# A two-block layer with a mixture of 32 experts: the order of the output projection, the first expert and its ten weight buffers

## The reference

```python
mixed = merged @ w_o
h = _layer_norm(DEEPNORM_ALPHA * h + mixed, ln1_g, ln1_b)       # 512 x 1024
pg = softmax(h @ w_rg + b_rg)                                    # 4 groups
grp = argmax(pg)
le = (h @ w_re + b_re).reshape(512, 4, 8)[token, grp]            # 8 experts of the group
top_v, top_i = top_k(le, 2)                                      # 2 experts a token
for each block of rows of one expert e (32 experts, 1024 -> 512 -> 1024):
    y = (silu(xb @ w1[e]) * (xb @ w3[e])) @ w2[e]
out[token] += gate * y
```

## Time and profile before

| | |
|---|---|
| median of 3 runs | 2123.84 us (2122.33 to 2124.23) |
| the profiled execution | 2123.43 us, of which the profile's span is 2121.6 us |
| PE, DVE, ACT, POOL busy | 92%, 44%, 31%, 21% of the span |
| the experts, from the first gather to the last weight | about 732 to 1226 us |

### The profile page before, as it was taken

The page is one execution under the profiler, slowest core; times in us unless marked ns, Lnnn a source line. Parts: engine busy times, 40 slices in busy tenths (PEclk is TensorE's granted clock), DMA queues, the critical chain, the costliest instruction groups (busy, mean ns, idle before and its releaser), DMA issues.

```text
span 2121.6 us, 23001 instructions
## 1 busy us (share of the span) xinstructions
PE 1958.5 (92%) x9509; PEld 1427.4 (67%) x9509; DVE 930.6 (44%) x1398; ACT 667.6 (31%) x993; POOL 444.4 (21%) x311
## 2 busy tenths in 40 slices
PE   7999999999999699887978899998889999999999
PEld 6788878788878533333333358876767787888887
DVE  6866385724436612111111155445546883222342
ACT  4644532424333101000000133541238752222221
POOL 5542221424325111111111023211003200000121
PEclk9998999999999799988999899999999999999999
DMA  4872462213334699999999964111111134323211
GB/s 165 271 190 61 99 120 40 89 51 80 80 123 189 247 392 403 404 403 397 416 408 411 423 238 139 60 50 50 50 50 40 59 133 136 119 79 119 80 60 40
DMA packets 108310, 369.47 MB, mean 174 GB/s; under 512 B 10682, under 2 KB 43708, under 8 KB 95912
## 3 DMA queue, kind: packets, MB, share of 16 engines
q1 hardware_dynamic: 97456, 343.58, 46.0%
q0 software_dynamic: 8240, 19.00, 2.6%
q10 hardware_dynamic: 2504, 5.35, 0.7%
HBM read 345.03 MB, written 29.15 MB: 176 GB/s over the span
## 4 chain that ended last, share of the span: by engine, by line
PE 75%; DVE 12%; issue 5%; ACT 5%; DMA 2%; POOL 0%; SPq 0%; DVEq 0%; POOLq 0%; ACTq 0%
PE ps L278 71%; PE ps L282 3%; DVE ST L262 3%; PE ps L2210 2%; DVE H L268 1%; ACT ST L274 1%; ACT M L274 1%; ACT L274 1%; DVE ST L1088 1%; DVE WL L262 1%; DVE BG L262 0%; DMA ypad<-BG,yrow 0%; DVE ML L262 0%; DMA BG<-h1d,toki 0%; DVE H L265 0%
## 5 line engine op out<-in xcount | busy, mean ns | idle before, releaser
L278 PE MATMUL ps<-XH,WS 128*128 128x512 f32 x704 | 216.7, 389 | 0.0
L278 PE MATMUL ps<-W,BG 128*64 128x512 f32 x448 | 159.1, 642 | 22.0 <-issue 22.0
L278 PEld LDWEIGHTS ps<-XH,WS 128*128 128x128 f32 x704 | 132.2, 188 | 27.3
L2318 DVE COPY BG<-ps 128x512 f32<-128x512 f32 x32 | 22.1, 692 | 285.5 <-PE ps L278 285.5
L272 ACT ACTIVATE BG<-ps 128x512 f32<-128x512 f32 x48 | 28.6, 595 | 372.3 <-PE ps L2210 336.6
L278 PE MATMUL ps<-ST,BG 128*64 128x512 f32 (+2 forms) x384 | 139.5, 572 | 6.2 <-issue 4.5
L278 PE MATMUL ps<-XL,WS 128*128 128x512 f32 x352 | 137.0, 389 | 1.4 <-DVE XL L262 1.4
L278 PE MATMUL ps<-X2H,GV 128*128 128x512 f32 (+1 forms) x512 | 130.1, 343 | 0.0
L278 PE MATMUL ps<-HTH,WL 128*128 128x512 f32 x448 | 115.6, 395 | 0.0
L278 PE MATMUL ps<-WS,HH 128*128 128x512 f32 x352 | 108.5, 389 | 0.9 <-DVE WS L262 0.9
L278 PE MATMUL ps<-M,BG 128*64 128x512 f32 (+1 forms) x288 | 100.0, 525 | 8.1 <-ACT ST L272 6.4
(11 more groups left out here) (400 smaller groups left out, 4436.2 us busy)
## 6 DMA issues: line engine op xcount, KB each, us to landing
W<-in_w SPq DMA_DIRECT2D x28, 2048.0 KB, 40.7
W<-in_w_in SPq DMA_DIRECT2D x27, 2048.0 KB, 10.1
ST<-in_w SPq DMA_DIRECT2D x19, 2048.0 KB, 42.1
W<-in_w_ffn_in SPq DMA_DIRECT2D x22, 1024.0 KB, 7.7
BG<-in_w SPq DMA_DIRECT2D x10, 2048.0 KB
U<-in_w SPq DMA_DIRECT2D x10, 2048.0 KB, 39.5
...
```

Of the source, the lines that this page charges most:

```text
L278: return p.e.matmul(o, lhsT=l, rhs=r, start=start, stop=stop, skip_group_check=True)
L2318: v.e.tensor_copy(hs[j], t.at).then_inc(t.drained)
```

## The change

It has five parts.

1. Order in `p_merge`: the half y = 0 of all four tiles is computed first, then y = 1. The logits of tiles 0 and 1 now stand inside the last two results, and the turn of a tile follows its y = 1 half. ACT does all copies of turned tiles. The norm of the last tile is written in two halves, and its first transposes wait for the first half alone.
2. Buffers: the fourth buffer (slot 3) is now the region `BG` 8 to 15, which held the split half 0 of `w_o`, instead of `U`, which takes the experts' small tiles. The order of buffers and of the sources is changed so that loads 4 and 5 (now w1 and w3 of expert 1; load 3 is w2 of expert 0) wait only for the last y = 0 result.
3. Expert 0's rows: no gather. DVE makes, ahead of everything else that follows the ranks, a one-hot matrix of expert 0's tokens (`oh0`), and PE gets the transposed rows by 32 float32 products of `H` with it.
4. Order in `p_experts`: eh(0), the list for the overflow rows, et(0), ex(1), ey(0), and only then eh(1).
5. `occupy`: 2, 6 and 1 products of constants ahead of the last logits, the ranks and expert 0's rows.

```diff
@@ -212,7 +212,7 @@
         b_rows = [nc.dram_tensor(f"b_rows{y}", (32, P), F32).ap() for y in range(2)]
-        Wt += [U.rearrange("p a b -> p (a b)"), M.rearrange("p a b -> p (a b)")]
+        Wt += [BG[:, 8:16, :].rearrange("p a b -> p (a b)"), M.rearrange("p a b -> p (a b)")]
         Wt += [ST[:, 2:10, :].rearrange("p a b -> p (a b)"), HT.rearrange("p a b -> p (a b)")[:, 0:4096]]
@@ -342,7 +342,9 @@
                 srcs += [wrows(a["w1"][0, x], 8), wrows(a["w3"][0, x], 8)]
-            if x:
+            if x == 0:
+                srcs.append(wrows(a["w2"][0, 0], 4))
+            elif x > 1:
                 srcs.append(wrows(a["w2"][0, x - 1], 4))
@@ -354,7 +356,7 @@
-        EXP_SLOTS = (5, 1, 7, 2, 0, 3, 4, 6, 8, 9)
+        EXP_SLOTS = (5, 1, 7, 2, 3, 0, 4, 8, 6, 9)
         EXP_LAST = (5, 7, 3, 4, 6, 1)
...
@@ -419,7 +421,11 @@
             v.wait_ge(*v.now)
-            stt(o, o, rs[:, i:i + 1], rows[:, br, :], MUL, ADD).then_inc(ln_hi)
+            if halves:
+                stt(o[:, 0:512], o[:, 0:512], rs[:, i:i + 1], rows[:, br, 0:512], MUL, ADD).then_inc(ln_lo)
+                stt(o[:, 512:], o[:, 512:], rs[:, i:i + 1], rows[:, br, 512:], MUL, ADD).then_inc(ln_hi)
+            else:
+                stt(o, o, rs[:, i:i + 1], rows[:, br, :], MUL, ADD).then_inc(ln_hi)
         def v_ln_high(X, u, i, gr, br, rows_in, rows=rows):
@@ -439,9 +445,12 @@
-        def p_turn(name, X, u, i, banks):
-            p.wait_ge(ln_hi, 4 * u + i + 1)
+        def p_turn(name, X, u, i, banks, first=None):
             for h in range(2):
+                if h or first is None:
+                    p.wait_ge(ln_hi, 4 * u + i + 1)
+                else:
+                    p.wait_ge(*first)
                 t = B.tile((name, i, h), banks[h])
@@ -1737,7 +1746,7 @@
             for m in range(2):
-                t = B.tile(("wo", m, 0), 2 * m)
+                t = B.tile(("wo", m, 0), m)
                 room(t)
@@ -1758,27 +1767,26 @@
-            for m in range(NT):
+            for m, y in [(2, 0), (3, 0)] + [(m, 1) for m in range(NT)]:
                 z = slice(m * P, (m + 1) * P)
-                for y in range(m < 2, 2):
-                    hi, lo = cols8(WO[y]), cols8(WL[slot[20 + y]])
-                    t = B.tile(("wo", m, y), (2 * m + y) % 4)
-                    room(t)
-                    for k in range(8):
-                        p.wait_ge(sp_hi, job["wo", y, k // 2] + 1)
-                        mm(t.at, MH[:, k, z], hi[:, k, :], start=k == 0, stop=False)
-                        mm(t.at, ML[:, k, z], hi[:, k, :], start=False, stop=False)
-                    for k in range(8):
-                        p.wait_ge(*split_done(("wo", y, k // 2)))
-                        i = mm(t.at, MH[:, k, z], lo[:, k, :], start=False, stop=k == 7)
-                    i.then_inc(t.filled)
-                    w_used[20 + y] = [t.full()]
-                    if m and y == (m == 1):
-                        p_turn("h1", H, 2, m - 1, (4 + 2 * (m % 2), 5 + 2 * (m % 2)))
-                if m > 1:
+                hi, lo = cols8(WO[y]), cols8(WL[slot[20 + y]])
+                t = B.tile(("wo", m, y), m)
+                room(t)
+                for k in range(8):
+                    p.wait_ge(sp_hi, job["wo", y, k // 2] + 1)
+                    mm(t.at, MH[:, k, z], hi[:, k, :], start=k == 0, stop=False)
+                    mm(t.at, ML[:, k, z], hi[:, k, :], start=False, stop=False)
+                if y and m > 1:
                     p_logits(m - 2)
+                for k in range(8):
+                    p.wait_ge(*split_done(("wo", y, k // 2)))
+                    i = mm(t.at, MH[:, k, z], lo[:, k, :], start=False, stop=k == 7)
+                i.then_inc(t.filled)
+                w_used[20 + y] = [t.full()]
+                if y and m:
+                    p_turn("h1", H, 2, m - 1, (4 + 2 * (m % 2), 5 + 2 * (m % 2)))
             p_logits(2)
-            p_turn("h1", H, 2, 3, (4, 5))
+            p_turn("h1", H, 2, 3, (4, 5), first=(ln_lo, 5))
             p_logits(3)
         def p_logits(i):
@@ -1786,6 +1794,8 @@
             p.wait_ge(c_r, 128)
+            if i == NT - 1:
+                occupy(t, 2)
             for h in range(2):
@@ -1827,12 +1837,11 @@
                 v_wo(m, 0)
-                if m:
-                    turned_out(v, "h1", m - 1, 0)
+            for m in range(NT):
+                if m > 1:
+                    v_logits(m - 2)
                 v_wo(m, 1)
                 v_ln2(m)
-                if m > 1:
-                    v_logits(m - 2)
         def v_wo(m, y):
@@ -1845,7 +1854,7 @@
         def v_ln2(m):
...
             v.e.bn_aggr(mv[:, m, :], bnst[:, m, :, :].rearrange("p j k -> p (j k)")).then_inc(ln_var)
-            v_ln_steps(H, 2, m, 0, 1, rows2)
+            v_ln_steps(H, 2, m, 0, 1, rows2, halves=m == NT - 1)
         def g_merge():
@@ -1896,6 +1905,7 @@
                 if m:
+                    turned_out(s, "h1", m - 1, 0)
                     turned_out(s, "h1", m - 1, 1)
@@ -1906,6 +1916,8 @@
         yrow_done = sem("y_rows")
+        x0_m, x0_q = BG[:, 16, 172:176], BG[:, 16, 168:172]
+        oh0 = BG[:, 16, 256:512].rearrange("p (i r) -> p i r", i=4)
         row_hot, blk_tok = sem("row_one_hot"), sem("block_tokens")
...
@@ -1940,14 +1953,23 @@
         def p_router():
...
             room(t)
+            occupy(t, 6)
             p.wait_ge(ms_done, 1)
...
             z.then_inc(t.filled)
+            t = B.tile(("ex", 0), 0)
+            room(t)
+            occupy(t, 1)
+            p.wait_ge(row_hot, 1)
+            for k in range(8):
+                for i in range(NT):
+                    z = mm(t.at[:, k * BLK:(k + 1) * BLK], H[:, i, k::8], oh0[:, i, :], start=i == 0, stop=i == NT - 1)
+            z.then_inc(t.filled)
             t = B.tile("tok", 7)
             room(t)
-            p.wait_ge(row_hot, 1)
+            p.wait_ge(row_hot, 2)
             for n in range(8):
@@ -1965,7 +1987,7 @@
         def s_router():
-            act(BG[:, 8:12, :], cst[:, 0:512].unsqueeze(1).to_broadcast([P, 4, 512]), ACT.Copy, scale=0.0).then_inc(rt_out)
+            act(U[:, 0:4, :], cst[:, 0:512].unsqueeze(1).to_broadcast([P, 4, 512]), ACT.Copy, scale=0.0).then_inc(rt_out)
             s.wait_ge(rt_in, 1)
@@ -2035,6 +2057,8 @@
             ts(v, io64[:, 32:64], io32, 32.0, None, ADD, None).then_inc(v.up())
+            v.wait_ge(*v.now)
+            ts(v, io64p, io64, 1.0, None, ADD, None).then_inc(v.up())
             v.e.memset(mfb[:, 128:160], 0.0).then_inc(v.up())
@@ -2043,14 +2067,22 @@
+            tt(v, x0_m, mk[:, 0, :, 0], mk[:, 1, :, 0], ADD).then_inc(v.up())
+            t = B["rank"]
+            R = t.at[:, 0:128].rearrange("p (i n) -> p i n", i=4)
             for c in range(2):
                 ts(v, mkt[:, 0, c, :, :], mk[:, c, :, :], cst[:, C_TOK:C_TOK + 1], None, MUL, None).then_inc(v.up())
+                if c:
+                    v.wait_ge(*v.now)
+                    tt(v, oh0, io64p.unsqueeze(1).to_broadcast([P, 4, BLK]), x0_q.unsqueeze(2).to_broadcast([P, 4, BLK]),
+                       ALU.is_equal).then_inc(row_hot)
                 tt(v, mkt[:, 1, c, :, :], mk[:, c, :, :],
                    tile1.unsqueeze(2).to_broadcast([P, 4, 32]), MUL).then_inc(v.up())
-            t = B["rank"]
-            v.wait_ge(*t.full())
+                if c == 0:
+                    v.wait_ge(*v.now)
+                    v.wait_ge(*t.full())
+                    stt(x0_q, R[:, :, 0], 1.0, x0_m, ADD, MUL).then_inc(v.up())
             sc = RT[:, 7, 0:256].rearrange("p (c i n) -> p c i n", c=2, i=4)
-            R = t.at[:, 0:128].rearrange("p (i n) -> p i n", i=4)
             tt(v, sc, mk, R.unsqueeze(1).to_broadcast([P, 2, 4, 32]), MUL).then_inc(v.up())
@@ -2170,7 +2202,7 @@
-        flatK, flatV = [x.rearrange("p a b -> p (a b)") for x in (Kr, Vr)]
+        flatK, flatV = [x.rearrange("p a b -> p (a b)") for x in (U, Vr)]
         NR = 4
@@ -2195,17 +2227,17 @@
         def src13(b, n):
-            return N_EXP + (3 * b - 1 + n if b else n)
+            return N_EXP + (3 * b - 1 + n if b > 1 else 3 * b + n)
         def src2(b):
-            return N_EXP + (4 + 3 * b if b < NE - 1 else 3 * NE - 1)
+            return N_EXP + (2 if b == 0 else 4 + 3 * b if b < NE - 1 else 3 * NE - 1)
         def p_expert_x(b):
             j = b % NR
-            p.wait_ge(c_xg[j], 16 * (b // NR + 1))
             t = B.tile(("ex", b), b % 2)
             room(t)
+            p.wait_ge(c_xg[j], 16 * (b // NR + (j > 0)))
             for k in range(8):
@@ -2246,16 +2278,19 @@
         def p_experts():
-            p_expert_x(0)
             for b in range(NE):
                 p_expert_h(b)
+                if b == 0:
+                    p_over_rows()
+                    p_expert_t(0)
                 if b + 1 < NE:
...
                 if b == 0:
-                    p_over_rows()
+                    p_expert_y(0)
+                    continue
```

(14 more changed lines are left out.)

7 lines of the change are left out of this document (4 added, 3 removed).

## The result

The changed kernel takes 2130.20 us (median of 20 runs, 2124.57 to 2135.22), the kernel before 2123.89 (20 runs, 2121.75 to 2131.25): a ratio of 1.0027, interval 1.0019 to 1.0035. The prediction, 2122.2 in 2117.0 to 2128.0, had the sign wrong and its range missed the time. The profiled execution took 2134.2 us, one of the slowest of its 20, so its rows are compared stage by stage. The interval excludes 1, but about a third of the difference is not traced to a cause in what follows.

What follows compares the result with a forecast made beforehand. The expert weight stream was taken as the bound. Load 14 moves from 767.8 to 766.2, held by expert 1's first products: 1.6 us gained, 2123.43 to 2121.8, plus 0.4 for the median: 2122.2, range 2117.0 to 2128.0.

Steps and rivals of the forecast that it cites:

- the price of expert 0's row products: Expert 0's rows on PE: 64 instructions take 7.5 us at the high clock (14.0 at the low), ending at 738.2.
- A strided stationary operand may add some: Expert 0's row products on PE: a caveat that the stride of H may cost time, given no size.
- case C: Slower: expert 0's 64 row instructions fall on the low clock; 2127.2 or 2129.5 us; loss if ending after 739.8; chance 0.28.
- The chain from the end of the row products to the end of expert 1's w1 and w3: From 738.2 to 766.2: 28.0 us, or 28.8 if expert 0's w1 and w3 products run low too.
- the two groups behind idle time: ey(0) and eh(1) on PE: start at the low clock after idle time, costing 2.4 us (bounds 0 and some 3).
- The head start: Loads 4 and 5 go out early, load 6 at 714.0; load 14's turn at 760.0, not 767.8: at most 7.8 us gained.
- load 11's release: Expert 0's products free loads 11 and 12 at 745.9 (before 751.79); gains nothing by itself, as the queue drains before load 14.
- The forecast's own rule for load 14: Weight stream: load 14's turn comes 16.0 us after load 11's issue, or at its release by expert 1's first products.
- DVE's row work: On DVE after the token list: 9.2 us ahead of the copy of expert 0's first result, which ends at 748.7.
- C's worst end: Low-clock row products started at 730.7: a loss of 5.7 us, 2129.5; chance of slower beyond 0.2% put at 0.10.
- D: Waits shrink, by shorter DVE row work or an earlier list; the 7.8 us ceiling is reached, 2116.0 us; chance 0.08.
- A: Clock high throughout, or the two late groups keep it: 2119.9 to 2117.5 us; chance 0.27.

Runs made afterwards that it cites:

- no_constants: The change without its nine products of constants (2, 6 and 1 become 0): 2129.45 us, ratio 1.0024 to before.
- blocks_no_constants: rows_by_blocks without the nine products of constants: 2130.64 us, ratio 1.0029 to before.
- early_loads_alone: The kernel before with only the change's new w_o order and buffers; gather, expert order and weight load order as before: 2127.03 us, ratio 1.0016.
- contiguous_rows: The change with the row products' stationary operand from 128 neighbouring columns of H, not every eighth; weights not matched: 2124.81 us, ratio 1.0004.
- the swapped kernels with the old order: The change with one-hot stationary, H moving, old expert and load orders: 2121.72 us; contiguous H, matching weights: 2120.08; that without constants: 2122.53.
- rows_old_order: The change with PE's old order of experts, its order of weight loads kept: 2132.39 us, ratio 1.0033 to before.
- gather_old_order: The change with parts 3, 4 and 5 undone, leaving the w_o order and the buffers: 2130.20 us, ratio 1.0030 to before.
- swapped_by_blocks: The change with one-hot stationary, H moving contiguously, expert 0's w1 and w3 loaded to match, old expert and load orders: 2120.08 us, ratio 0.9987.
- rows_by_blocks: The change with the row products' stationary operand from neighbouring columns and expert 0's w1 and w3 loaded to match: 2122.08 us, ratio 0.9991.
- blocks_list_inside: rows_by_blocks with the old expert and weight load orders and the token list behind the first 16 row instructions: 2125.23 us, ratio 0.9998.

## Why the prediction was wrong

**The step that failed** is the price of expert 0's row products: "I take the high price ... 7.5", from products whose stationary operand has neighbouring columns. "A strided stationary operand may add some" stood beside it without a number and was in no bound. They took 15.5 us. The stride adds some 8 us at the high clock (0.24 us each, the rate of the first 2.6 us of the change, makes 15.4 for 64, against 7.36) and 1.6 at the low one (15.46 against 13.88). I asked only which of the two clock levels would hold; the stride gives nearly the low price at either. The break-even of case C was an end at 739.8; measured is 745.8, and 1.95 us of that is the later load 1.

The Trainium skill, SBUF — State Buffer, section Door 1: The DMA port swizzle, says that accesses within one 16-byte line of SBUF run at full rate and each one that crosses to a new line pays, so that 4 float32 elements are the free stride. Here the stride is 8 elements, and the trace agrees that it costs, with 333 ns for a weight load in place of 192, and 1097 for a moving operand in place of 598. By that page alone the strided price would have been a rival with a chance of its own.

**The case.** With the 1.95 us of the later load 1 taken off, the row products started at 728.35 and ended at 743.9. The forecast had them start at 730.7, behind constants at the low clock; the granted clock was 1.00 again from 723 on, ahead of the six constants. So this step was 2.3 us better than forecast, and the products' length 8.0 us worse. Case C for that start says 742.4 for their end and 2127.2 us; measured is 2130.20. Its sign and its low clock are right, but its cause is not: the clock did fall, at 733, with PE busy, and no_constants shows that this cost the strided row products nothing, while blocks_no_constants shows that without the stride it would have cost them 6.5 us. The chain from the end of the row products to the end of expert 1's w1 and w3 was put at 28.0 to 28.8 us; measured 745.81 to 772.94, 27.1. In it the two groups behind idle time took 11.89 us where the high clock gives 3.6 + 7.0: 1.3 more, not 2.4. With the measured terms the forecast's sum is 743.9 + 27.1 = 771.0 against 767.8, 3.2 us lost, and the first profiles of the two kernels differ by 3.4 in this stage.

The Trainium skill, TensorE: Matmul & The Clock Gate, section HAM oscillation, has the low clock come behind waits of PE. The trace agrees where PE waits 2.89 us ahead of ey(0): the granted clock is 1.00 from 758 to 760 and 0.54 from 762 to 764. In the change it also came inside a stretch of 15.5 us in which PE never waited.

**The head start**, a ceiling of 7.8 us, failed by itself as well: early_loads_alone is 0.16% slower than before. The ceiling let loads 6 to 13 run from 714.0 without a pause. But load 11 waits for expert 0's w1 and w3 products, and in early_loads_alone the queue is empty ahead of it (750 to 754), as it is ahead of load 10 in the change (741 to 746). I had taken load 11's release as worthless, since "the queue drains ahead of load 14". In the table load 11 and the stage go together: 99 to 103 us and 555 to 558.5, 111 and 564 to 565.5. Load 14's issue does not tell these apart, for it is 120.8 us behind load 1 in early_loads_alone and 121.5 in contiguous_rows, whose stages are 564.1 and 557.4.

The forecast's own rule for load 14 fits: its turn is its release, or 16.0 us behind load 11's issue, whichever is later. Counted from load 1 that turn is 125.5 us before and 128.7 in the change. From the turn to `H<-h1d` there are 434 to 437 us in twelve of the seventeen profiles, both of before and both of the change among them. In the swapped kernels with the old order load 13 is released together with load 14, so its 5.3 us count as well, and with them these three have 435 to 436. (Counted in the same way rows_old_order and gather_old_order have 433; early_loads_alone has 437.4.) For early_loads_alone the rule gives 126.7, already 1.2 us later than before: the 2117.6 expected of it had left load 11 out. And where the queue hardly runs empty the head start is there: swapped_by_blocks, with a DMA share of 1.00 from 734 to 756, has a stage of 554.8 us, 6.5 and 3.8 below the two of before. That the gather is slower in early_loads_alone was in no sum.

**Partly luck.** rows_by_blocks is the change at the forecast price (7.36 us for 7.5), and its 2122.08 is the forecast's 2122.2. The kernel contiguous_rows, with the same row time, took 2124.81, so the match is closer than such runs can tell. The chain of rows_by_blocks from the end of the row products to the end of eh(1) is also the forecast's 28.0 us (735.24 to 763.26), but by another wait: ahead of ex(1) it is the gather of expert 1's rows, 9.56 us, and not DVE's row work. The forecast named no such wait.

**What held.** Loads 4 and 6 at 686.8 and 714.05 (687 and 714), the 1.95 us taken off; one-hot ready at 728.35, the figure that the prediction gives for a high clock; the six constants at the high clock and off the path (12 instructions in 2.84 us); DVE's row work of 9 us ending just ahead of expert 0's copy; 2.89 us of idle time ahead of ey(0) (2.8); load 14 at expert 1's end and not in the queue. The 1.8 us of idle time ahead of et(0) did not come, as the row products ended later. That the clock differs between runs of one kernel shows in their mean granted clock: over the change's twenty runs it goes from 0.972 (2124.57 us) to 0.965 (2134.26). But the change's 10.7 us of scatter over twenty runs are no sign of it alone, for before has 9.5. The chance of 0.10 for slower by over 0.2% went with C's worst end alone; and 0.24 for faster is a little more than D and half of A, 0.215.

**Open.** The stage explains some 4 us of the 6.3 between the medians (564 to 565 against 559 to 561); the rest lies in the scatter of the profiles, or is not found. Why the clock held in rows_by_blocks and fell in blocks_list_inside was not settled. Whether the old orders with neighbouring columns and a high clock reach 2116 was not seen.
